# Channel mixer with the two halves of its activations paired in one moving operand, and the samples taken out to gathered expert rows

## The reference

```python
q = (x @ w_q).reshape(8, 2, 128)                 # 8 heads, 2 halves
s = einsum('hcd,chkd->hck', q, sub_keys)         # 128 keys per half
sv, si = top_k(s, 16)                            # 16 best of each half
cand = sv[:, 0, :, None] + sv[:, 1, None, :]     # 256 pairs per head
top_s, ci = top_k(cand, 16)
e = i1 * 128 + i2                                # 16 of 16384 experts per head
gate = softmax(top_s)
act = gelu(einsum('hed,d->he', u[e], x))         # exact gelu
y = einsum('he,hed->d', gate * act, v[e])
```

## Time and profile before

| | us |
|---|---|
| median of 3 runs | 2504.04 (2503.45 to 2508.36) |
| the profiled execution, span from first to last instruction | 2507.1 (no other time of it is known) |
| TensorE matmul busy | 2330.1 |
| TensorE weight loads busy | 2217.5 |
| VectorE busy | 1713.6 |
| GpSimd busy | 1669.8 |
| ScalarE busy | 1112.0 |
| DMA | 370 MB, 148 GB/s over the span |

### The profile page before, as it was taken

How to read it: one execution, slowest core, us unless ns; L and a number is a source line. 1 busy time by engine, 2 the same in 40 slices (tenths; PEclk the granted TensorE clock), 3 DMA queues, 4 the chain that set the end, 5 groups by cost and what they waited for, 6 DMA issues and landing times. The chain is left out here.

```text
span 2507.1 us, 46304 instructions
## 1 busy us (share of the span) xinstructions
PE 2330.1 (93%) x19024; PEld 2217.5 (88%) x19024; DVE 1713.6 (68%) x2773; ACT 1112.0 (44%) x1893; POOL 1669.8 (67%) x716
## 2 busy tenths in 40 slices
PE   6977978999999999999979875899999999999998
PEld 5957858999999999999979722899999999999998
DVE  4776553795678268888868376349767762888887
ACT  4512234455554444444446412344555444444443
POOL 4714016687666788888867544758766668888885
PEclk9978988999999999999989977899999999999999
DMA  4410013454444555555535443445544445555553
GB/s 156 153 52 34 35 44 135 144 185 160 144 144 144 169 184 178 184 178 184 179 123 169 157 151 109 133 137 163 176 146 147 145 147 182 180 182 181 181 182 131
DMA packets 102226, 370.27 MB, mean 148 GB/s; under 512 B 15392, under 2 KB 15744, under 8 KB 98816
## 3 DMA queue, kind: packets, MB, share of 16 engines
q1 hardware_dynamic: 102016, 367.30, 45.4%
HBM read 352.67 MB, written 14.58 MB: 146 GB/s over the span
## 5 line engine op out<-in xcount | busy, mean ns | idle before, releaser
L355 POOL TENSOR_TENSOR weights_halves<-weights_raw,weights_halves 128x1024 fp32r<-128x1024 f32 x638 | 1541.6, 2419 | 571.1 <-ACT weights_halves L347 570.8
L347 ACT CAST weights_halves<-weights_raw 128x1024 fp32r<-128x1024 f32 x638 | 669.9, 1051 | 936.2 <-PE peer L378 482.6
L860 DVE TENSOR_TENSOR gated<-acts,gated 128x264 fp32r<-128x264 f32 x256 | 615.3, 2405 | 127.5 <-ACT gated L742 127.5
L378 PE MATMUL peer<-ffn_in_hi,weights_halves 128*128 128x264 f32 x4608 | 650.7, 288 | 14.9 <-ACT ffn_in_hi L271 14.9
L378 PEld LDWEIGHTS peer<-ffn_in_hi,weights_halves 128*128 128x128 f32 x4608 | 590.9, 189 | 22.0 <-issue 16.6
L364 PE MATMUL peer<-gated,weights_halves 128*128 128x264 f32 x2048 | 583.2, 285 | 0.0
L362 PE MATMUL peer<-gated,weights_halves 128*128 128x264 f32 x2048 | 581.2, 284 | 0.0
L363 PE MATMUL peer<-gated,weights_halves 128*128 128x264 f32 x2048 | 579.9, 283 | 0.0
L363 PEld LDWEIGHTS peer<-gated,weights_halves 128*128 128x128 f32 x2048 | 385.9, 188 | 0.0
L362 PEld LDWEIGHTS peer<-gated,weights_halves 128*128 128x128 f32 x2048 | 385.4, 188 | 0.0
L364 PEld LDWEIGHTS peer<-gated,weights_halves 128*128 128x128 f32 x2048 | 384.4, 188 | 0.0
(11 more groups left out here) (465 smaller groups left out, 2359.3 us busy)
## 6 DMA issues: line engine op xcount, KB each, us to landing
weights_raw<-in_up SPq DMA_DIRECT2D x256, 512.0 KB, 3.5
weights_raw<-in_down SPq DMA_DIRECT2D x256, 512.0 KB, 3.5
weights_raw<-in_ssm_w_in SPq DMA_DIRECT2D x40, 512.0 KB, 3.4
weights_raw<-in_w_q SPq DMA_DIRECT2D x32, 512.0 KB, 3.4
weights_raw<-in_ab_w_in SPq DMA_DIRECT2D x30, 512.0 KB, 3.5
weights_raw<-in_ssm_w_out SPq DMA_DIRECT2D x16, 512.0 KB, 3.5
states<-in_ssm_in SPq DMA_DIRECT2D x8, 1024.0 KB, 7.4
ssm_sample<-states SPq DMA_DIRECT2D x8, 1024.0 KB, 4.8
```

Source lines behind the costliest of these rows:

```text
L347: act.copy(self.halves[:, 0, slot, :], self.raw[:, slot, :]).then_inc(self.hi_made, 1)
L355: pool.tensor_tensor(self.halves[:, 1, slot, :], self.raw[:, slot, :], self.halves[:, 0, slot, :].bitcast(F32), ALU.subtract).then_inc(sel ...
L378: ins = pe.matmul(out, self.halves[:, half, n % RING, at], both[side], start=start and half == 0 and side == 0 and k == 0, stop=stop and h ...
L860: core.gated_lo.inc(dve.tensor_tensor(a_lo[:, j % RING, :], acts[:, j, :], a_hi[:, j % RING, :].bitcast(F32), ALU.subtract))
```

## The change

In the up stage from tile 40 on, and in the down stage, the upper and lower activations of the 256 prompt tokens lie side by side as one moving operand of 512 columns. Upper weights are multiplied with the pair in one matmul of 512 columns, into both halves of a PSUM bank; lower weights with the upper activations, 256 columns, into the second half of the bank. A tile then is 8 matmuls of 512 and 8 of 256. The bank's second half (the cross terms) has to be added to the first: in the up stage ScalarE copies it to SBUF and VectorE adds it in the bank before gelu; in the down stage VectorE adds both halves to x at the end. Up tiles 0 to 39 keep three matmuls, now of 256 columns.

The 8 samples leave the up and down stages. Their 128 chosen experts per head (8 tokens x 16) are gathered as rows of u, and later of v, by an indirect DMA from GpSimd, 8 + 8 per layer, with one dot product or one weighted sum of 128 x 1024 on VectorE for each, in the down stage, one per six tiles. The 64 remaining quads of prompt tokens are spread over 84 tiles (40 to 122). The lower weights of all tiles stay on GpSimd (the new set on_dve is empty).

The diff, cut to its core:

```diff
-QUADS = T // 4
-EXP_TILE = 22
-TURN_TILE = 36
-FIRST_GATED = 38
-GATED_AHEAD = 120
+QUADS = SEQ // 4
+EXP_TILE = 24
+TURN_TILE = 38
+FIRST_GATED = 40
+FIRST_PAIRED = FIRST_GATED
+QUAD_TILES = 84
+GATED_AHEAD = 124
+FIRST_DOT = 10
+FIRST_WEIGHTED = 64
+SAMPLE_STEP = 6
+SAMPLES_AFTER = 3
+GELU_TILE = FIRST_DOT + SAMPLE_STEP * PEER_HEADS
+QUAD_AT = {FIRST_GATED + q * QUAD_TILES // QUADS: q for q in range(QUADS)}
...
+    def pair_product(self, pe, out, n, cols, pair, start, stop):
         hi, lo = self.halves[:, 0, n % RING, cols], self.halves[:, 1, n % RING, cols]
+        pe.matmul(out, hi, pair, start=start, stop=False, skip_group_check=True)
+        return pe.matmul(out[:, SEQ:2 * SEQ], lo, pair[:, 0:SEQ], start=False, stop=stop, skip_group_check=True)
+    def pair_products(self, pe, out, n, pairs, cols):
+        pe.wait_ge(self.hi_made, n + 1)
+        for k, (pair, at) in enumerate(zip(pairs, cols)):
+            pe.matmul(out, self.halves[:, 0, n % RING, at], pair, start=k == 0, stop=False, skip_group_check=True)
+        self.await_lo(pe, n)
+        for k, (pair, at) in enumerate(zip(pairs, cols)):
+            ins = pe.matmul(out[:, SEQ:2 * SEQ], self.halves[:, 1, n % RING, at], pair[:, 0:SEQ], start=False,
+                            stop=k == len(pairs) - 1, skip_group_check=True)
+        return ins
...
             def _(sp):
                 ring.load_to(sp, first + RING + 1)
                 core.load(sp, keys, sub_keys)
+                sp.wait_ge(core.norm_hi.sem, norm.hi0 + KC)
+                halves_paired.inc(sp.dma_start(pairs[:, :, 0:SEQ].bitcast(F32), h_hi[:, :, 0:SEQ].bitcast(F32)), 16)
+                sp.wait_ge(core.norm_lo_pool.sem, norm.pool0 + KC // 2)
+                sp.wait_ge(core.norm_lo_dve.sem, norm.dve0 + KC // 2)
+                halves_paired.inc(sp.dma_start(pairs[:, :, SEQ:2 * SEQ].bitcast(F32), h_lo[:, :, 0:SEQ].bitcast(F32)), 16)
                 ring.load_to(sp, end + RING)
...
             def _(pool):
+                ring.make_lo(pool, down + RING)
+                pool.wait_ge(core.sample_copied.sem, kinds0 + 1)
+                pool.wait_ge(ring.multiplied, down)
+                for n in range(2 * PEER_HEADS):
+                    ring.make_lo(pool, down + 2 * RING + SAMPLE_STEP * n)
+                    if n >= GATHER_SLOTS:
+                        pool.wait_ge(gather_used.sem, used0 + n - GATHER_SLOTS + 1)
+                    head = n % PEER_HEADS
+                    gathered[n % GATHER_SLOTS].inc(pool.indirect_dma_start(
+                        out=slots[:, n % GATHER_SLOTS, :], out_offset=None, in_=(up_rows, down_rows)[n // PEER_HEADS],
+                        in_offset=bass.IndirectOffsetOnAxis(ap=expert[:, head:head + 1], axis=0)), 16)
                 ring.make_lo(pool, end + RING)
...                                                                # TensorE, query tiles
+                    if s == 0:
+                        pe.wait_ge(rows_copied.sem, rows_copied0 + 1)
+                        for k in range(KC):
+                            last = pe.matmul(row_banks[k // 4][:, (k % 4) * P:(k % 4 + 1) * P],
+                                             sample_rows[:, k * P:(k + 1) * P], core.ident, start=True, stop=True)
+                        rows_spread.inc(last)
...                                                                # TensorE, after a block of the last down tile
+                        if j == KEYS - 1 and d == SAMPLES_AFTER:
+                            pe.wait_ge(cross_added.sem, crossed0 + 4)
+                            pe.wait_ge(gather_used.sem, used0 + 2 * PEER_HEADS)
+                            for k in range(KC):
+                                summed = pe.matmul(sums[1][:, k * DEC:(k + 1) * DEC], weighted_sum[:, columns[k]],
+                                                   core.row_token, start=True, stop=True)
+                            sample_ready.inc(summed)
...                                                                # ScalarE, up tile j
-                    ring.make_hi(act, up + j + RING + 1)
+                    if j < FIRST_PAIRED:
+                        ring.make_hi(act, up + j + RING + 1)
...
                     act.wait_ge(ring.multiplied, up + j + 1)
+                    if j >= FIRST_PAIRED:
+                        cross_copied.inc(act.copy(cross, bank[:, SEQ:2 * SEQ]))
+                        ring.make_hi(act, up + j + RING + 1)
+                        act.wait_ge(halves_added.sem, added0 + j - FIRST_PAIRED + 1)
...                                                                # ScalarE, down tile j
+                    if j == GELU_TILE:
+                        act.wait_ge(gather_used.sem, used0 + PEER_HEADS)
+                        core.gelu_made.inc(act.activation(expert_act, expert_act, ACT.Gelu))
...                                                                # VectorE
+                def add_halves(j):
+                    dve.wait_ge(cross_copied.sem, copied_cross0 + j - FIRST_PAIRED + 1)
+                    bank = projected[(SETS + j) % RING]
+                    halves_added.inc(dve.tensor_tensor(bank[:, 0:SEQ], bank[:, 0:SEQ], cross, ALU.add))
...
+                def dot(head):
+                    n = head
+                    dve.wait_ge(gathered[n % GATHER_SLOTS].sem, gathered0[n % GATHER_SLOTS] + 16 * (n // GATHER_SLOTS + 1))
+                    slot = slots[:, n % GATHER_SLOTS, :]
+                    gather_used.inc(dve.tensor_tensor_reduce(slot, slot, sample_rows, 1.0, 0.0, ALU.mult, ALU.add,
+                                                                  expert_act[:, head:head + 1]))
+                def weigh(head):
...
+                        gather_used.inc(dve.scalar_tensor_tensor(weighted_sum, slot, expert_act[:, head:head + 1],
+                                                                      weighted_sum, ALU.mult, ALU.add))
...
                 for j in range(FIRST_GATED, KEYS):
+                    quad = QUAD_AT.get(j)
+                    if j >= FIRST_PAIRED:
+                        add_halves(j)
+                    if j > FIRST_GATED:
                         gate_tile(j)
+                    if quad is not None:
+                        apply(quad, j)
+                        if quad + 2 < QUADS:
+                            build(quad + 2)
                     if j == GATED_AHEAD:
                         for t in range(RING):
                             make_gated_lo(t)
-                for j in range(RING, KEYS):
-                    make_gated_lo(j)
+                for j in range(KEYS):
+                    if j + RING < KEYS:
+                        make_gated_lo(j + RING)
+                    if j >= FIRST_DOT and (j - FIRST_DOT) % SAMPLE_STEP == 0 and (j - FIRST_DOT) // SAMPLE_STEP < PEER_HEADS:
+                        dot((j - FIRST_DOT) // SAMPLE_STEP)
...                                                                # weigh likewise, from tile 64 on
                 for d in range(KC):
...
-                    core.residual_made.inc(dve.tensor_tensor(x[:, d, :], sums[d][:, 0:T], x[:, d, :], ALU.add))
+                    add_to_x = Link(dve, cross_added)
+                    add_to_x(dve.tensor_tensor(x[:, d, 0:SEQ], sums[d][:, SEQ:2 * SEQ], x[:, d, 0:SEQ], ALU.add))
+                    last = dve.tensor_tensor(x[:, d, 0:SEQ], sums[d][:, 0:SEQ], x[:, d, 0:SEQ], ALU.add)
+                    (cross_added if d <= SAMPLES_AFTER else core.residual_made).inc(last)
+                    if d == SAMPLES_AFTER:
+                        dve.wait_ge(sample_ready.sem, ready0 + 1)
...                                                                # adds the samples' sums to x
```

More of the change, by code:

```diff
@@ L21 @@
 SSM_SLOTS = 3
+GATHER_SLOTS = 3
 class Count:
@@ L86, in __init__ @@
         self.ids_turned = Count(nc, "ids_turned")
+        self.gathered = [Count(nc, f"gathered{i}") for i in range(GATHER_SLOTS)]
         self.gates_built = Count(nc, "gates_built")
@@ L651, in score @@
                     core.head_scored.inc(last)
-                def tile_product(tile, out):
-                    ring.products(pe, out, tile, [(h_hi[:, k, :], h_lo[:, k, :]) for k in range(KC)],
-                                  [slice(k * P, (k + 1) * P) for k in range(KC)], start=True,
-                                  stop=True, norm=norm if tile == first else None).then_inc(ring.multiplied, 1)
+                columns = [slice(k * P, (k + 1) * P) for k in range(KC)]
                 for s in range(SETS):
@@ L660, in _ @@
                         pe.wait_ge(core.query_copied.sem, copied0 + s - RING + 1)
-                    tile_product(first + s, projected[s % RING][:, 0:T])
+                    ring.products(pe, projected[s % RING][:, 0:T], first + s,
+                                  [(h_hi[:, k, :], h_lo[:, k, :]) for k in range(KC)], columns, start=True, stop=True,
+                                  norm=None if s else norm).then_inc(ring.multiplied, 1)
```

(22 more changed lines are left out.)

190 lines of the change are left out of this document (127 added, 63 removed).

## The result

The changed kernel takes 2524.06 us (median of 4 runs, 2518.86 to 2527.99), the kernel before 2506.2 on the same chip (4 runs, 2503.45 to 2508.72): ratio 1.0071, 95% interval 1.0053 to 1.0088. It is 0.7% slower; the forecast was 2469, faster. The profiled execution has a span of 2520.4 us and took 2522.16.

What follows compares the result with a forecast made beforehand. TensorE, busy for 93% of the span, was taken as the bound. Terms summed to -17.8 us a layer, -35.6 for two, +1 at the start: 2504.0 - 34.6 = 2469, with an 8-in-10 range of 2390 to 2528.

Steps and rivals of the forecast that it cites:

- A paired tile: Up tiles from 40 and down: 8 matmuls of 512 and 8 of 256 columns take 2.69 us, 0.22 less.
- the third rival: Matmuls cost by the column: a paired tile takes 2.82 us, pairing saves only 0.09, whole kernel 2486; chance 11%.
- Up tiles 0 to 39: First part of up stage: matmuls of 256 columns and two quads fewer of gate building, -4.8 us per layer.
- up 40 to 127: Rest of up stage: the loop over ScalarE and VectorE runs late behind TensorE, 295.6 us, -10 per layer.
- Down: Down stage: 341.6 us on TensorE plus 18.7 left of 16 sample steps gives 360.3, -10 per layer.
- GpSimd becomes the bound: Down stage: a sample step costs 4.35 us as lower activations miss a turn; +20.7 per layer, kernel 2546; chance 19%.
- Query stage: Query stage: eight turning matmuls, a wait for ScalarE's copy of sample columns and SP's pair copies, +2 us per layer.
- tail: Additions to x: two dependent ones per block, ending 8.2 us after the first block instead of 3.0; +5 per layer.
- My own mark: Down stage: the forecast called itself wrong if this took more than 375 us.

Runs made afterwards that it cites:

- the run with memsets: Changed kernel with GpSimd setting the slot to ones in place of each gather, dot products and weighted sums kept; 2489.68 us, ratio 0.9922 to the kernel before.
- the run in which no turn is lost: Changed kernel with GpSimd, after each gather, waiting for VectorE's lower activations ahead of each of its next three subtractions; 2486.89 us, ratio 0.9911 to before.

## Why the prediction was wrong

The sum said -34.6 on the span; it came out as 2520.4 - 2507.1 = +13.3. The step that failed is in the down stage: that a gather costs only what it takes of GpSimd's time, and that VectorE gets its turn between GpSimd's operations each time. In its place 32 of 32 lower activations lost two turns or three behind a gather, worth 37 us. A second term, the paired tile, was mis-sized. By its steps:

*A paired tile* was mis-sized: 2.69 forecast, 2.80 measured, inside its bounds and near the upper one. 256 columns were right (118); 512 columns take 232 ns where I took 218. TensorE alone needs 127 x 0.11 = 14 us more per layer in down for it. In my sum only some 4 of them count, since a longer tile leaves GpSimd more to spare: the third rival, with 2.82, has -5.9 for down where I had -10. My step was to take 512 columns midway between a rate and a fixed cost; the earlier trace rows are of plain fp32, which takes 222 ns where fp32r takes 121 for the same 264 columns, and were a poor neighbour. The rival of a rate per column was right on TensorE (0.453 ns a column at 512, 0.461 at 256). Three slips of mine change little: the midway of 215.3 and 224.3 is 219.8 and not 218 (a tile of 2.70), the bound of -13 for up tiles 0 to 39 comes to -10 at 112 ns each, and 2.92 over 24 matmuls is 121.7 ns and not 121.2. I also misread the Trainium skill (TensorE: Matmul & The Clock Gate, Back-to-back issue gap): the page gives N/2.4 + 2.5 ns for a single matmul by itself and says that a stream with weight loads departs from it, so the trace's 121.2 does not disagree with the page.

*Up tiles 0 to 39*: -2.0 instead of -4.8; *up 40 to 127*: -10.1 for -10, but not for my reason. The loop over ScalarE and VectorE that I had as the bound sets the period nowhere but at one tile, 123 (3.82): a quad tile takes 3.55 and the others 2.79 on TensorE, which is its own time, 88 x 2.79 + 64 x 0.77 = 294.8 of 295.7, and it is idle for 0.11 in this stretch. Only ScalarE's copies fall behind in the last 15 or so tiles. So -10.1 is luck: a dearer tile and a loop that stayed hidden, as the third rival had it, cancelled.

*Down* decided the sign: +18.4 and +14.4 for -10 and -10. The floor is 356.1 instead of 341.6. The steps cost 32.5 and 28.5 over it, where I had 18.7. The prices that I put together were good (gather 0.97 for 0.95; dot products and memsets together 15 and 13 per layer, in the run with memsets). What failed is the assumption behind them, that VectorE gets its turn between GpSimd's operations each time, as in the earlier trace rows, where no DMA from GpSimd comes in between. Behind a gather it doesn't: 32 of 32 requests lost two turns or three. In the changed kernel this cost stands in the place of the dot product's, not on top of it: the dot product fits into the idle time that the lost turns make.

*The rival "GpSimd becomes the bound"* had the direction and half of the mechanism: lower activations miss turns. It laid that to the dot product (3.1 per step as the point where it decides); the runs lay it to the gather, at 1.77 per long tile, and with a TensorE floor 14 us higher 1.77 was enough. It had 19%.

*How much each was worth.* The third rival, which has the tile at 2.82 and the steps at my price, came to 2486; the run in which no turn is lost takes 2486.89. By that, of the 55 us between 2469 and 2524.06 some 17 are the tile and 37 the lost turns. With the dearer tile alone the change would still have been faster, by 18 in the rival's sum; the lost turns took more than that. That the two numbers meet to the microsecond is luck, since the rival's up stages and tails are off by several us in both directions.

*Query stage* +1.8 and +1.2 (forecast +2), *tail*: the additions to x run for 7.4 (1273.87 to 1281.28 on VectorE's timeline) instead of 2.96, forecast 8.2 from the first block. Up to the next stage's weights the tail of layer 1 costs 5.6, and after layer 2 the end of the kernel comes 2.4 later, where I had 5 for each. A stretch of layer 2's token mixer, which the change doesn't touch, is 3.9 shorter in the changed kernel and in all its variants; I had nothing for it, and why is open. The first gather of layer 1 takes 1.12, its request loses three turns (8.11), and TensorE, idle for 4.1, goes on at a granted clock of 0.53 from 907.0 to 910.5, near the 1.2 GHz level, where it had 1.00 before: this tile is 4.2 longer than those of other steps.

My own mark, down over 375 us, is what gave the sign; the lower weights and activations appeared on TensorE's list of waits, as written.

What stays open: why GpSimd keeps the turn behind a gather. That it does is shown by the gathers taken out, replaced and yielded behind, and by the boundaries counted; whether any DMA from GpSimd does it, and how long it would last, is open too. Nothing here looks into GpSimd.

## What to carry to other kernels

Where two engines take turns at a shared resource, the price of an added operation is not its own time alone: look at who is queued at the next boundaries, and test one gather or one long operation in the stage before placing sixteen. A stage that looks free on an engine because it waits hides the turn order; when the tile leaves little over the two engines' turns (here 2.80 against the 2.56 of the earlier trace rows), move one of them off the resource (here 1.23 on the other engine for 2.40; 2466.55 us) rather than arrange the turns (2486.89). For a width of matmul that no row has, price it by the column from the nearest rows of the same type: here that was right within 2% (0.459 ns a column from 264 columns, 0.453 at 512).

## What the runs showed of the hardware that was not expected

- Behind an indirect DMA of 128 rows GpSimd runs its two-operand subtractions without letting VectorE's two-operand operation in between: 64 of 64 requests that came in a gather, with GpSimd's next subtraction released, lost two turns or three (changed kernel and the run without dot products). At the boundaries counted above VectorE got in at 0 of 124 behind a gather and at 160 of 160 otherwise.
- A gather takes 0.97 of GpSimd on the mean in the changed kernel, and 1.68 (0.94 to 1.92) where VectorE runs subtractions of 1024 columns (lower weights on VectorE): the 26 that began while such a subtraction was running took 1.81 to 1.92, five that began before it 0.94. The Trainium skill (SBUF — State Buffer, Who interferes with whom) supposes that such an operation leaves the writing of descriptors alone; these gathers do not fit that. Whether it is their descriptors that wait or the reading of their list of rows is not shown.
- fp32r matmuls, each with its own weights: 232 ns from start to start at 512 columns, 118 at 256 between those (changed kernel), 120 at 256 among themselves (512 columns as two of 256), 121.5 at 264 (kernel before, 370.2 us for 127 tiles of 24).
